# A two-block sequence model on one core: the order of weight splits and HGRN steps in the mixers

## The chip, the cores and the metric

One NeuronCore of a Trainium2 chip runs one launch of the kernel; the other cores are idle. The metric is the device time of that launch in microseconds. In the profile, PE is TensorE's matmul row, PEld its weight loads, DVE is VectorE, ACT is ScalarE, SP is SyncE, whose queue issues the DMAs. All arithmetic is fp32 in effect.

## The reference

The input is 256 tokens of width 1024. The reference applies a first block and then a second one. The first block has two layers, each a mixer and a gated feed-forward network; the second has a sparse-attention layer and a sliding-window layer, each with a feed-forward network as well. The change touches the mixer of the first block, which runs twice. It is, cut to what matters:

```python
p = rmsnorm(x) @ w_in                 # qkv, z, beta, a, hq, hf (2 directions), hi, gates
q, k, v = silu(dwconv(qkv)); q, k = l2norm(q) * 128**-0.5, l2norm(k)      # 4 heads of 128
# gated delta rule, forward and backward, chunks of tokens:
t_inv = inverse(eye + strict_lower(beta * k @ k.T * decay))
o_dn  = scan(t_inv @ (v * beta), t_inv @ (k * beta * exp(gc)), q @ k.T * decay, ...)
# HGRN2, forward and backward: S_t = diag(f_t) S_{t-1} + (1 - f_t) i_t^T, o_t = S_t^T q_t
o_hg  = scan(silu(hq), kk, hi, cumsum(logf))
merged = sigmoid(gate_dn) * (norm(o_dn) * silu(z) @ w_branch_dn) + sigmoid(gate_hg) * (norm(o_hg) * silu(hgate) @ w_branch_hg)
x = x + merged @ w_out
```

## The kernel before, in words

The kernel is written by hand, one instruction stream for each engine; each engine works strictly in the order written, and the streams meet at semaphores. TensorE counts finished groups in `P`, ScalarE its instructions in `A`, VectorE in `V`. PSUM is a ring of 8 banks (`Banks`): a group of matmuls takes the bank that was given back longest ago and waits until the results of its former owner have been read out of it.

**Weights.** All weights are streamed in tiles of 128 x 2048 fp32 (1 MB), in the order of `plan`. A tile passes through three steps. SP loads it into one of the raw buffers `RAW`. ScalarE casts it into a high half `WH` (`cp(half(WH, i), raw(i))`, L1100, recorded at the helper's line L1082). VectorE subtracts the high half from the raw tile, which gives the low half `WL` (L1687, recorded at L1659). TensorE then forms three products for each tile (high x high, high x low, low x high), in `feat`: 48 matmuls, about 6 us. `WH` and `WL` have three slots (`NWS`); the cast of tile i waits until TensorE is through with tile i - 3. On ScalarE and VectorE one call of `chunk()` does the next cast or subtraction in line, wherever in the stream it is written; ScalarE is one tile ahead of VectorE.

`RAW` has three slots, but from tile 16 to tile 29 of a mixer only two, since the third holds the gate projections `zg`. So tile 16 goes where tile 13 was, tile 17 where 15 was, tile 18 where 16 was, tile 19 where 17 was, and so on. SP issues the loads in order, each of them after the cast and the subtraction of the tile that it overwrites:

```python
elif j is not None:              # j = slot_former[i]
    w.wait_ge(*A["w hi", j])
    w.wait_ge(*V["w lo", j])
e.dma_start(raw(i), plan[i][0]).then_inc(*s_raw[slot[i]].up("raw", i))
```

The tiles of a mixer: 0 to 5 are qkv, 6 is narrow, 7 and 8 are `hq`, 9 to 12 are `f 0` to `f 3`, 13 and 14 are `it`, 15 to 18 are the projections `zp 0` to `zp 3`, from 19 on come the gates. The second mixer's tiles are the same plus 68.

**The head of the mixer.** TensorE projects `hq`, `f 0` and `f 1`; then come the small product `gc`, two groups of transposes `vt 0` and `vt 1`, and then four heads h, each with `kq h` (products of k and q with k), two groups `row h d`, which need `gB` and then a projection (`f 2`, `f 3`, `it 0`, `it 1`). The group `vt 1` is the next owner of the bank of `gc`. On ScalarE the inverse norms (`l2`, `rq`) are followed by a cast, by the logarithms of the forget gate (`logs(0)`) and the copies of `vt`. VectorE copies `gc`, forms `gB`, scales q and k (`unit(0)`, `unit(1)`), subtracts a tile, and then, head by head, masks (`dm`), forms the pairs, and runs `rest(h)`, a cumulative sum over the forget gate, whose last operations wait for ScalarE's `rest(h)`.

**The levels.** After fence f2 come six levels of a recursive triangular inverse on four groups g4 of 128 x 512 elements: TensorE multiplies (`y`), ScalarE copies, TensorE multiplies (`z`), and VectorE (to level 4) or ScalarE places the result with predicated copies and 32 x 32 transposes. Woven into these levels are 16 steps of HGRN, n = 0 to 15. Step n on VectorE is `hg_step(n)`: a predicated copy of the matmul result n (odd n only), the exponents of step n + 2 (`hg_exp`, two operations) and the product for step n + 1 (`hg_mul`, one or two operations), between which ScalarE takes the exponential. TensorE has a pair of matmul groups `hg` for odd n. `HG_STEPS` says how many steps lie in each level: two between and after the groups, any others at the end of the level. Levels 1 to 4 begin with a projection: TensorE runs `zp 0` before level 1 and `zp 1`, `zp 2`, `zp 3` at the ends of levels 1, 2 and 3; VectorE scales it in `zproj`. Tiles 17 to 21 are cast and tiles 16 to 20 subtracted in the calls of `chunk()` in this part.

Of the kernel before, what the change touches and what calls it, by code (L numbers as in the profile page):

```python
# [120 lines left out]
def program(nc, a):  # L121
    P_AT, P_W = par_layout()
    ctx = ExitStack()
    with ctx:
# [162 lines left out]
        XIv, XTv = (x.rearrange("p (g h n) -> p g h n", g=4, h=4) for x in (XI, XT))  # L287
        YBv = [y.rearrange("p (h n) -> p h n", h=4) for y in YBs]
        attv = att.rearrange("p (h s t) -> p h s t", h=4, s=2)
        HG_STEPS = (2, 2, 3, 3, 3, 3)  # L290
        HGI = [(kind, lv) for lv in (7, 0, 1, 2, 3, 4, 5, 6) for kind in range(2)]
        TM = [YBv[0], YBv[1]]
        vtv = vt.rearrange("p (j h n) -> p j h n", j=2, h=4)
# [780 lines left out]
        def scalar(e):  # L1074
# [12 lines left out]
            def waits(*pairs):  # L1087
                for s in pairs:
                    w.wait_ge(*s)
# [44 lines left out]
            def mixer(l):  # L1134
# [52 lines left out]
                def logs(c):  # L1187
                    E_, L1, L2 = HT[c % 2]
                    w.wait_ge(*V["f in", st, c])
                    act(E_, E_, ACT.Exp, "f exp", st, c)  # L1190
                    waits(A["f exp", st, c], *(f0 if c < 2 else [V["k out", st, c - 2]]))
                    act(L1, E_, ACT.Ln, "f l1", st, c, bias=1.0)
                    w.wait_ge(*V["lb"])
                    for j in range(2):
                        i = 2 * c + j
                        s1 = slice(j * 256, j * 256 + 256)
                        act(L2[:, s1], E_[:, s1], ACT.Ln, "f l2", st, c, bias=1.0, scale=LB[:, l * 8 + i:l * 8 + i + 1])

                def rest(c):
                    E_, L1, L2 = HT[c % 2]  # L1200
                    w.wait_ge(*V["f log", st, c])
                    act(L1, L1, ACT.Exp, "f inv", st, c, scale=-1.0)

                logs(0)
                for j in range(2):
                    w.wait_ge(*P["ps", st, "vt", j])
                    cp(vt[:, j * 512:j * 512 + 512], ps[st, "vt", j][:, :], "vt", st, j, of=ps.out(st, "vt", j))
                for h in range(4):
                    for d in range(2):
                        c = 4 * d + h  # L1210
                        dm = Dm[c % 2 + 2 * d]
                        major, minor = (slice(128, 384), slice(0, 128)) if d == 0 else (slice(0, 256), slice(256, 384))
                        waits(V["dm", st, h, d], V["bg", st])
                        act(dm[:, major], ps[st, "row", h, d][:, 0:256], ACT.Exp, "dm", st, h, d, bias=bg[:, d, c:c + 1],
                            of=ps.out(st, "row", h, d))
                        act(dm[:, minor], dm[:, minor], ACT.Exp, "dm", st, h, d, bias=lb_[:, 1 - d, c:c + 1])
                    if h == 0:
                        rest(0)
                    if h == 3:
                        for g4 in range(4):  # L1220
                            cp(XTv[:, g4], ident.unsqueeze(1).to_broadcast([128, 4, 128]), "ident", st, g4)
                    chunk()
                    if h >= 2:
                        c = h - 2
                        waits(P["ps", st, "it", c], V["rsT", st])
                        for j in range(2):
                            e.mul(v3(it, 2)[:, j, c * 256:c * 256 + 256], v3(ps[st, "it", c][:, :], 2)[:, j], rsT[:, j:j + 1]) \
                                .then_inc(*A.up("it", st, c, of=ps.out(st, "it", c)))
                    if h < 3:
                        logs(h + 1)  # L1230
                        rest(h + 1)
                A.note("f2", st)
                f2 = fence("f2", st)
                waits(*f2)

                def placed(out, src, kind, lv, *key, of):
                    for o, x in places(out, src, kind, lv):
# [49 lines left out]
                for lv in range(1, 7):  # L1287
                    for g4 in range(4):
                        dn_y(g4, lv)
                    if lv == 1:  # L1290
                        hg_diag()
                    hg_mm(n)
                    hg_exp(n + 2)
                    dn_z(0, lv)
                    dn_z(1, lv)
                    hg_mm(n + 1)
                    hg_exp(n + 3)
                    dn_z(2, lv)
                    dn_z(3, lv)
                    for m in range(2, HG_STEPS[lv - 1]):  # L1300
                        hg_mm(n + m)
                        hg_exp(n + m + 2)
                    n += HG_STEPS[lv - 1]
                    if lv < 5:
                        chunk()
                A.note("f3", st)
                f3 = fence("f3", st)
# [346 lines left out]
        def vector(e):  # L1654
# [117 lines left out]
            def mixer(l):  # L1772
# [37 lines left out]
                def forget(c):  # L1810
                    E_ = HT[c % 2][0]
                    waits(P["ps", st, "f", c, 0], *(f0 if c < 2 else [V["k out", st, c - 2]]))
                    stt(v3(E_, 2), v3(ps[st, "f", c, 0][:, :], 2), -1.0, rs2, ALU.mult, ALU.mult, "f neg", st, c, of=ps.out(st, "f", c, 0))
                    w.wait_ge(*V["f neg", st, c])
                    ts(E_, E_, 40.0, None, ALU.min, None, "f in", st, c)
# [16 lines left out]
                def unit(n):  # L1832
                    sx, sk = slice(n * 512, n * 512 + 512), slice(1024 + n * 512, 1536 + n * 512)
                    w.wait_ge(*A["rq", st, n])
                    stt(q_[:, sx], q_[:, sx], 128.0 ** -0.5, rq[:, sx], ALU.mult, ALU.mult, "q", st, n)
                    w.wait_ge(*A["rq", st, n + 2])
                    tt(k_[:, sx], k_[:, sx], rq[:, sk], ALU.mult, "k", st, n)
# [16 lines left out]
                tt(g_, gw2[:, :, 8:16], nea.unsqueeze(1).to_broadcast([128, 2, 8]), ALU.mult, "g", st)  # L1854
                ts(lb_, gw2[:, :, 0:8], -1.0, None, ALU.mult, None, "ln beta", st)
                forget(0)
                w.wait_ge(*P["ps", st, "gc"])
                cp(gc, v3(ps[st, "gc"][:, 0:16], 2), "gc", st, of=ps.out(st, "gc"))
                waits(V["gc", st], V["ln beta", st])
# [1 line left out]
                waits(V["g", st], *f0, *(P["ps", st, "l2", n] for n in range(4)))  # L1861
                for j in range(2):
                    cp(gB[:, j], g_[:, j, :].unsqueeze(2).to_broadcast([128, 8, 128]), "gB", st)
                unit(0)
                unit(1)
                chunk()
                e.memset(bb[:, :, 0:1], 0.0).then_inc(*V.up("bb0", st))

                for h in range(4):
                    if h < 3:  # L1870
                        forget(h + 1)
                    for d in range(2):
                        c = 4 * d + h
                        p, dm = ps[st, "row", h, d], Dm[c % 2 + 2 * d]
                        minor, ms, at, m1 = (slice(0, 128), slice(128, 256), 1, "MF") if d == 0 else \
                            (slice(256, 384), slice(0, 128), 0, "MB")
                        waits(P["ps", st, "row", h, d], V["gc", st], V["k", st, 1], *([V["pair", st, h - 2, d]] if h > 1 else []))
                        stt(dm[:, minor], p[:, ms], gc[:, at, c:c + 1], cn(m1), ALU.subtract, ALU.min, "dm", st, h, d,
                            of=ps.out(st, "row", h, d))
                    for d in range(2):  # L1880
                        c = 4 * d + h
                        dm, pg, pq = Dm[c % 2 + 2 * d], ps[st, "kk", h], ps[st, "kq", h]
                        o = slice(128, 512) if d == 0 else slice(0, 384)
                        b = slice(3, 6) if d == 0 else slice(0, 3)
                        waits(A["dm", st, h, d], P["ps", st, "kq", h])
                        stt(AT6[:, b, h], v3(pg[:, o], 3), -1.0, v3(dm, 3), ALU.mult, ALU.mult, "pair", st, h, d, of=ps.out(st, "kk", h))
                        tt(QKv[:, d, h], pq[:, o], dm, ALU.mult, "pair", st, h, d, of=ps.out(st, "kq", h))
                    if h == 0:
                        rest(0)
                    if h < 3:  # L1890
                        chunk()
                        rest(h + 1)
# [88 lines left out]
                tt(ZR[2], kk_[:, 0:1024], kk_[:, 1024:2048], ALU.add, "k sum", st)  # L1981
                hg_exp(0)
                hg_exp(1)
                hg_mul(0)
                chunk()

                def zproj(c):
                    scaled(zg[:, c * 512:c * 512 + 512], (st, "zp", c, 0), "zp", st, c)
# [6 lines left out]
                for lv in range(1, 7):  # L1995
                    if lv < 5:
                        zproj(lv - 1)
                    hg_step(n)
                    dn_z(0, lv)
                    dn_z(1, lv)  # L2000
                    hg_step(n + 1)
                    dn_z(2, lv)
                    dn_z(3, lv)
                    for m in range(2, HG_STEPS[lv - 1]):
                        hg_step(n + m)
                    n += HG_STEPS[lv - 1]
                    if lv < 5:
                        chunk()
                V.note("f3", st)
                f3 = fence("f3", st)  # L2010
# [646 lines left out]
```

## Time and profile before

| | |
|---|---|
| median of 3 runs | 1728.71 us (1727.83 to 1730.08) |
| the profiled execution | 1728.71 us, span 1726.9 us |
| TensorE busy | 95% of the span |
| VectorE busy | 72% |
| ScalarE busy | 56% |
| DMA | 246.11 MB, mean 143 GB/s |
| first mixer, head to level 6 | about 84 to 227 us |
| second mixer, the same | about 595 to 734 us |

The time of the execution lies 1.8 us above the span, which goes from the first to the last instruction. A row of the timeline has the start and the length in us, the engine, the line, the operation, the output and input by name (SA and SB are large scratch areas in SBUF, PS is PSUM, SM small vectors), the shapes, and the number of instructions of the same kind merged into it; in square brackets stands how long the engine was idle before it, and whose work ended the wait. Matmul rows overlap a little, since matmuls are pipelined.

### The profile page before, as it was taken

The numbers are of one execution on the slowest core, as the hardware profiler recorded it, in microseconds if no ns is written. First come the engines' busy times: TensorE is split into PE (matmuls) and PEld (weight loads), VectorE is DVE, ScalarE is ACT, GpSimd is POOL, SyncE is SP. The second block draws the span as 40 slices with busy tenths as digits, with TensorE's granted clock in tenths as the row PEclk, the third lists the DMA queues.
The fourth block names the chain that finished last, engine by engine and source line by source line (L and its number), as shares of the span: only waits on it lengthen the run. The fifth ranks groups of instructions, "written<-read, shape, count | busy, mean of one in ns | idle before, by whom it ended". The sixth has DMA issues, their size and how long they took to land.

```text
span 1726.9 us, 30663 instructions
## 1 busy us (share of the span) xinstructions
PE 1647.3 (95%) x13206; PEld 1597.1 (92%) x13206; DVE 1237.0 (72%) x1715; ACT 968.7 (56%) x1426; POOL 0.2 (0%) x4
## 2 busy tenths in 40 slices
PE   6999899999999999899999998999999998899997
PEld 6999899999999899899999996878999998799997
DVE  6889946777747789846777646766688748678863
ACT  6664455556536664565556542347577635567752
POOL 0000000000000000000000000000000000000000
PEclk9999999999999999999999999999999999999999
DMA  6421124455554312126555542520454543055551
GB/s 259 170 74 63 61 74 174 168 196 195 173 194 146 141 57 74 49 74 221 181 184 182 184 171 97 209 84 1 149 189 176 195 171 141 13 197 189 177 195 50
DMA packets 34983, 246.11 MB, mean 143 GB/s; under 512 B 3872, under 2 KB 4256, under 8 KB 5536
## 3 DMA queue, kind: packets, MB, share of 16 engines
q1 hardware_dynamic: 34848, 244.15, 39.8%
q8 instruction: 104, 1.70, 0.4%
q14 instruction: 31, 0.25, 0.0%
HBM read 243.09 MB, written 1.05 MB: 141 GB/s over the span
## 4 chain that ended last, share of the span: by engine, by line
PE 81%; DVE 13%; ACT 5%; issue 1%; DMA 0%; SPq 0%; DVEq 0%; ACTq 0%
PE PS L396 80%; DVE SA L1659 3%; DVE SB L1659 2%; ACT SB L1079 2%; DVE WL L1659 2%; DVE SB L1668 2%; ACT WH L1082 1%; DVE SB L1898 1%; PE PS L399 1%; DVE X L1659 1%; ACT XH L1122 0%; DVE SB L1663 0%; DMA RAW<-w_in 0%; DVE XL L1668 0%; DVE SA L1823 0%
## 5 line engine op out<-in xcount | busy, mean ns | idle before, releaser
L396 PE MATMUL PS<-XH,WH 128*128 128x256 f32 (+1 forms) x2536 | 725.3, 286 | 18.0 <-DVE WL L1659 17.3
L396 PE MATMUL PS<-XL,WH 128*128 128x256 f32 (+1 forms) x2536 | 717.6, 283 | 0.0
L396 PE MATMUL PS<-XH,WL 128*128 128x256 f32 (+1 forms) x2536 | 717.5, 283 | 0.0
L1082 ACT CAST WH<-RAW 128x2048 fp32r<-128x2048 f32 (+1 forms) x226 | 426.2, 1886 | 440.6 <-PE PS L396 391.5
L1659 DVE TENSOR_TENSOR WL<-RAW,WH 128x2048 fp32r<-128x2048 f32 (+1 forms) x226 | 510.9, 2261 | 159.5 <-ACT WH L1082 149.9
L396 PEld LDWEIGHTS PS<-XH,WH 128*128 128x128 f32 (+1 forms) x2536 | 484.6, 191 | 22.2 <-issue 18.1
L396 PEld LDWEIGHTS PS<-XL,WH 128*128 128x128 f32 (+1 forms) x2536 | 484.7, 191 | 2.6 <-issue 1.9
L396 PEld LDWEIGHTS PS<-XH,WL 128*128 128x128 f32 (+1 forms) x2536 | 484.6, 191 | 0.3
L396 PE MATMUL PS<-INH,WH 128*128 128x256 f32 x960 | 268.9, 280 | 1.1 <-DVE INL L1659 1.1
L396 PE MATMUL PS<-INH,WL 128*128 128x256 f32 x960 | 269.5, 281 | 0.0
L396 PE MATMUL PS<-INL,WH 128*128 128x256 f32 x960 | 267.0, 278 | 0.0
L396 PEld LDWEIGHTS PS<-INH,WH 128*128 128x128 f32 x960 | 180.5, 188 | 1.5 <-ACT INH L1082 1.5
L396 PEld LDWEIGHTS PS<-INL,WH 128*128 128x128 f32 x960 | 180.5, 188 | 0.0
L396 PEld LDWEIGHTS PS<-INH,WL 128*128 128x128 f32 x960 | 180.2, 188 | 0.0
L1659 DVE TENSOR_TENSOR SB<-PS,SM 128x512 f32<-128x512 f32 (+2 forms) x109 | 74.3, 682 | 85.5 <-PE PS L396 85.5
L1659 DVE TENSOR_TENSOR SB<-SB 128x512 f32<-128x512 f32 (+2 forms) x163 | 110.3, 677 | 12.3 <-ACT SB L1079 8.9
L396 PE MATMUL PS<-SA 128*128 128x128 f32 (+1 forms) x480 | 97.1, 346 | 18.8 <-DVE SA L1659 18.8
L396 PE MATMUL PS<-SB 128*128 128x128 f32 (+1 forms) x752 | 97.2, 285 | 9.9 <-ACT SB L1082 7.2
L1668 DVE SCALAR_TENSOR_TENSOR SB<-SB,PR 128x254 f32<-128x254 f32 (+2 forms) x212 | 95.6, 491 | 11.6 <-ACT SB L1079 8.0
L396 PEld LDWEIGHTS PS<-SB 128*128 128x128 f32 x752 | 91.0, 194 | 12.3 <-ACT SB L1082 11.3
L396 PEld LDWEIGHTS PS<-SA 128*128 128x128 f32 x480 | 70.0, 208 | 25.0 <-DVE SA L1659 16.2
L1082 ACT COPY SB<-PS 128x512 f32<-128x512 f32 (+4 forms) x156 | 68.3, 467 | 40.9 <-PE PS L396 39.1
(142 smaller groups left out, 1554.1 us busy)
## 6 DMA issues: line engine op xcount, KB each, us to landing
RAW<-w_in SPq DMA_DIRECT2D x52, 1024.0 KB, 4.9
RAW<-w_up SPq DMA_DIRECT2D x44, 1024.0 KB, 4.9
RAW<-f_in SPq DMA_DIRECT2D x44, 1024.0 KB, 4.8
RAW<-w_down SPq DMA_DIRECT2D x22, 1024.0 KB, 4.9
RAW<-f_out SPq DMA_DIRECT2D x22, 1024.0 KB, 4.8
RAW<-a_w_in SPq DMA_DIRECT2D x10, 1024.0 KB, 4.9
RAW<-w_out SPq DMA_DIRECT2D x8, 1024.0 KB, 4.9
RAW<-w_bdn SPq DMA_DIRECT2D x4, 1024.0 KB, 4.9
```

The lines of the kernel that those rows point to most:

```text
L396: return e.matmul(out, l, r, start=start, stop=stop, skip_group_check=True)
L399: return e.transpose(out, x, ident[0:k, 0:k])
L1079: e.activation(out, x, f, bias=bias, scale=scale).then_inc(*A.up(*key, of=of))
L1082: e.copy(out, x).then_inc(*A.up(*key, of=of))
L1659: e.tensor_tensor(out, x, y, op).then_inc(*V.up(*key, of=of))
L1668: e.scalar_tensor_tensor(out=out, in0=x, scalar=s, in1=y, op0=op0, op1=op1).then_inc(*V.up(*key, of=of))
L1898: e.copy_predicated(out, m, data).then_inc(*V.up(*key, of=of))
```

## The change

It moves calls within the streams of ScalarE and VectorE; no operation is added or removed on any engine. On ScalarE, `rest(0)` goes ahead of the `vt` copies, one `chunk()` goes from the end of level 4 to the place behind fence f2, and with it each cast from tile 18 to 21 is done one call earlier. On VectorE, `unit(0)`, `unit(1)` and their `chunk()` go ahead of the copy of `gc`, and `rest(0)` ahead of the loop over heads; `chunk()` comes before `hg_mul(0)` instead of after it, and the `chunk()` of the end of level 4 goes behind `zproj(0)` in level 1. `HG_STEPS` puts two steps into levels 3 and 4 and four into levels 5 and 6, on all three engines.

```diff
-        HG_STEPS = (2, 2, 3, 3, 3, 3)
+        HG_STEPS = (2, 2, 2, 2, 4, 4)
...
                 logs(0)                                     # ScalarE
+                rest(0)
                 for j in range(2):
                     w.wait_ge(*P["ps", st, "vt", j])
...
-                    if h == 0:
-                        rest(0)
...
                 f2 = fence("f2", st)
                 waits(*f2)
+                chunk()
...
                     n += HG_STEPS[lv - 1]
-                    if lv < 5:
+                    if lv < 4:
                         chunk()
...
                 forget(0)                                   # VectorE
+                unit(0)
+                unit(1)
+                chunk()
                 w.wait_ge(*P["ps", st, "gc"])
...
-                unit(0)
-                unit(1)
-                chunk()
                 e.memset(bb[:, :, 0:1], 0.0).then_inc(*V.up("bb0", st))
+
+                rest(0)
...
-                    if h == 0:
-                        rest(0)
...
                 hg_exp(0)
                 hg_exp(1)
+                chunk()
                 hg_mul(0)
-                chunk()
...
                         zproj(lv - 1)
+                    if lv == 1:
+                        chunk()
                     hg_step(n)
...
                     n += HG_STEPS[lv - 1]
-                    if lv < 5:
+                    if lv < 4:
                         chunk()
```

## Rows read from the trace of the kernel before

**Rows 1.** The page: busy us, share of the span and instructions of each engine.
```profile
PE 1647.3 (95%) x13206; PEld 1597.1 (92%) x13206; DVE 1237.0 (72%) x1715; ACT 968.7 (56%) x1426; POOL 0.2 (0%) x4
```

**Rows 2.** Windows: length, PE, PEld, DVE, ACT, POOL busy, clock, DMA share, GB/s.
```profile
150.00:175.00 25.00, 25.00 (x221) 25.00 (x220) 22.90 (x31) 9.78 (x13) 0.00 (x0) 1.00 0.24 85
191.90:226.70 34.80, 27.38 (x227) 27.05 (x227) 26.67 (x37) 18.03 (x37) 0.00 (x0) 0.95 0.10 31
699.90:734.40 34.50, 27.45 (x227) 27.07 (x227) 26.72 (x37) 18.04 (x37) 0.00 (x0) 0.95 0.09 31
```

**Rows 3.** SP's timeline and the DMA view (KB each, us to landing), 139 to 146 us: tile 18.
```profile
139.85 0.33 SPq L2498 DMA_DIRECT2D RAW<-w_in  x1
...
RAW<-w_in SPq DMA_DIRECT2D x1, 1024.0 KB, 4.7
```

**Rows 4.** VectorE's timeline: `hg_mul(0)`, tile 16, `zproj(0)`, one step; `hg_mul(0)`, second mixer.
```profile
136.27 0.69 DVE L1659 TENSOR_TENSOR SA<-SA 128x512 f32<-128x512 f32 x1
...
137.48 2.29 DVE L1659 TENSOR_TENSOR WL<-RAW,WH 128x2048 fp32r<-128x2048 f32 x1
139.69 0.69 DVE L1659 TENSOR_TENSOR RAW<-PS,SM 128x512 f32<-128x512 f32 x1
140.29 2.42 DVE L1659 TENSOR_TENSOR SA<-SA 128x512 f32<-128x512 f32 x3
...
645.59 0.69 DVE L1659 TENSOR_TENSOR SA<-SA 128x512 f32<-128x512 f32 x1
```

**Rows 5.** ScalarE's timeline, level 1: exponentials 0 and 1, and the cast of tile 18.
```profile
135.18 2.18 ACT L1079 ACTIVATE SA<-SA 128x1024 f32<-128x1024 f32 x2 [4.88 <-DVE SA L1659]
...
148.42 1.89 ACT L1082 CAST WH<-RAW 128x2048 fp32r<-128x2048 f32 x1
```

**Rows 6.** TensorE's timeline: level 1's first `z`, HGRN group 1, `zp 1`; the latter two, second mixer.
```profile
137.89 1.42 PE L396 MATMUL PS<-SB 128*128 128x128 f32 x8 [1.85 <-ACT SB L1082]
...
142.76 3.33 PE L396 MATMUL PS<-SA 128*128 128x128 f32 x16 [0.20 <-DVE SA L1659]
...
147.63 0.36 PE L396 MATMUL PS<-XH,WH 128*128 128x256 f32 x1
...
652.08 2.05 PE L396 MATMUL PS<-SA 128*128 128x128 f32 x16 [1.11 <-DVE SA L1659]
...
655.67 0.36 PE L396 MATMUL PS<-XH,WH 128*128 128x256 f32 x1
```

**Rows 7.** TensorE's timeline, head 0 of both mixers: `kq 0` and the start of `f 2`.
```profile
86.79 3.13 PE L396 MATMUL PS<-SA 128*128 128x256 f32 x8 [2.05 <-DVE SA L1659]
...
91.74 0.36 PE L396 MATMUL PS<-XH,WH 128*128 128x256 f32 x1
...
597.77 1.97 PE L396 MATMUL PS<-SA 128*128 128x256 f32 x8 [2.05 <-DVE SA L1659]
...
601.05 0.36 PE L396 MATMUL PS<-XH,WH 128*128 128x256 f32 x1
```

**Rows 8.** VectorE (`gc` copy, tile 12, head 1's `rest`) and ScalarE (last `rq`, both mixers).
```profile
83.85 0.17 DVE L1671 COPY SM<-PS 128x16 f32<-128x16 f32 x1 [2.22 <-PE PS L396]
...
87.77 2.28 DVE L1659 TENSOR_TENSOR WL<-RAW,WH 128x2048 fp32r<-128x2048 f32 x1
...
611.06 0.69 DVE L1659 TENSOR_TENSOR SB<-SB 128x512 f32<-128x512 f32 x1 [1.03 <-ACT SB L1079]
...
84.41 0.63 ACT L1079 ACTIVATE SB<-SB 128x512 f32<-128x512 f32 x1
...
594.61 0.63 ACT L1079 ACTIVATE SB<-SB 128x512 f32<-128x512 f32 x1
```

**Rows 9.** TensorE's timeline, first mixer: start of `zp 3`, HGRN groups 9 and 15.
```profile
176.99 0.36 PE L396 MATMUL PS<-XH,WH 128*128 128x256 f32 x1
...
196.68 3.65 PE L396 MATMUL PS<-SA 128*128 128x128 f32 x16 [4.77 <-DVE SA L1659]
...
224.68 2.02 PE L396 MATMUL PS<-SA 128*128 128x128 f32 x16 [0.87 <-DVE SA L1659]
```

## The prediction

> **What bounds the kernel now.** I read the page first: TensorE is busy for 1647.3 of 1726.9 us [rows 1], so only its 79.6 us of idle time can be won, and any new idle time is paid in full unless work is queued behind it. Then the table of windows; for the late levels of each mixer it has 34.80 us with 27.38 us busy and 34.50 us with 27.45 us busy, so 7.42 and 7.05 us idle, and a mean clock of 0.95, so part of each stretch ran at 1.2 instead of 2.4 GHz [rows 2]. The timelines say where: the heavy waits are one of 4.77 us for VectorE's product for HGRN group 9 and one of 0.87 us [rows 9]. Level 1 has waits too [rows 6], and so has the head of the mixer, 2.05 us each time [rows 7]. All the idle time that the edits can reach is in these three places. Between them TensorE has no wait (25.00 of 25.00 us busy in levels 2 and 3 [rows 2]), so a delay in one place reaches the end.
>
> **Part A, the head of the mixer (both `rest(0)`, the two `unit` calls and their `chunk()`).** Today TensorE waits 2.05 us for `k` of head 0 [rows 7]. With `unit(0)` first, `k` is ready in time: VectorE is idle there for 2.22 us, waiting for `gc` [rows 8]. But the low subtraction of tile 12 (2.28 us) now stands before the copy of `gc`. ScalarE ends the last `rq` at 84.41 + 0.63 = 85.04; then `k` (0.69, as the equally large operation in rows 4) gives 85.7, the subtraction 88.0, the copy of `gc` (0.17) 88.1 [rows 8]. The second `vt` transpose reuses the PSUM bank of `gc`, so TensorE waits for that copy and head 0's matmuls begin at about 88.5, not at 86.79. From there to the projection `f 2` it takes 601.05 - 597.77 = 3.28 us at the full clock (second mixer) and 91.74 - 86.79 = 4.95 us where the clock had fallen (first mixer) [rows 7]. At the full clock `f 2` would begin at 91.8 in the first mixer (before 91.74: +0.1) and, by the same sums from 594.61, at 602.0 in the second (before 601.05: +1.0). The new wait is some 3.8 us; waits of 2.05 us lowered the clock once in two cases [rows 7], waits of 4.77 us both times [rows 2, 9]. 3.8 is nearer to the second, so I add 4.95 - 3.28 = 1.67 us in both mixers: **+1.8 and +2.6, together +4.4 us**; bounds +1.1 and +4.4. VectorE cannot absorb it: its chain for head 1 waits for a cast that waits for `f 2`, with 1.03 us of idle time even now [rows 8]. The earlier `rest(0)` on both engines costs nothing more: its five VectorE operations only change places with the head-0 pairs, which TensorE needs two projections later, and the delayed `vt` copies are needed after `f 2`. If that cover were gone, it would be some 3 us.
>
> **Part B, level 1 (the new ScalarE `chunk()` behind fence f2, and on VectorE `chunk()` before `hg_mul(0)` and after `zproj(0)`).** The ScalarE call is the cast of tile 18. It waits for the load of tile 18. That load may start only when tile 16, which lies in the same raw buffer, has been cast and subtracted; today it is issued at 139.85, 0.08 us after the subtraction of tile 16 ends (137.48 + 2.29), and takes 4.7 us [rows 3, 4]. ScalarE now stands at this wait, and behind it in its queue are both first exponentials, the four `y` copies and the diagonal copies of level 1; TensorE's first level-1 `z` waits for the first `y` copy, VectorE's `hg_mul(0)` for the first exponential.
> Step by step, first mixer. VectorE is free for tile 16 where `hg_mul(0)` began, 136.27 [rows 4]; subtraction (2.29) to 138.5; load issued 138.6, landed 143.3; cast 1.89 to 145.2; the two exponentials 2.18 to 147.3 [rows 5]. Today `z` starts 137.89 - 137.36 = 0.53 us after the exponentials [rows 5, 6]: now at 147.8, **9.9 us later**. VectorE: first exponential 146.2, `hg_mul(0)` 1.3 to 147.5, `zproj(0)` to 148.1, the subtraction of tile 17, now in front, to 150.3, the next step (2.42) to 152.7 [rows 4]. HGRN group 1 starts at 152.7 instead of 142.76, **+9.9 us**, and it is this that decides when projection 1 starts. Second mixer: `hg_mul(0)` began at 645.59, so 152.7 - 136.27 = 16.4 gives 662.0 against 652.08, +9.9 [rows 4, 6].
> From group 1 to projection 1 it takes 655.67 - 652.08 = 3.59 us at full clock and 147.63 - 142.76 = 4.87 us at the low one [rows 6]. After an idle stretch of 12 us and another of 2 to 3 us the clock is low; a burst after a long wait lost 1.67 us in part A's rows, and I take this again. First mixer: 9.9 + 3.59 + 1.67 - 4.87 = +10.3. Second: 9.9 + 1.67 = +11.6. **Part B: +21.9 us**; bounds +18.6 (full clock) and +25.2 (the loss twice in each).
> Levels 2 and 3 give nothing back: TensorE is never idle there [rows 2]. ScalarE's casts 19, 20 and 21, now one level early, wait until the projection before has released their high buffer, but the `y` copies behind them are still in time for `z`, by about 1 us. If that were wrong, each level would lose up to 2 us.
>
> **Part C, levels 4 to 6 (`HG_STEPS`, `chunk()` only to level 3).** Let Z be the start of projection 3, 176.99 today; the last HGRN pair ends at 224.68 + 1.8 = Z + 49.5 [rows 9]. New order: level 4 has no group 9 and VectorE no third step and no subtraction. TensorE ends level 4 at Z + 14.8 (no wait). VectorE ends its level-4 placings of groups 2 and 3 at Z + 17.7 and 19.1, and `y` of level 5 waits for them: 1.6 us idle. Four `z` pairs and HGRN group 9 run to Z + 29.0 with no wait (its product is ready at Z + 22.3). Group 11 needs three VectorE steps after group 9 has been copied: at 2.42 us a step [rows 4] ready at Z + 31.1, 2.1 us idle. Level 6: `y` waits 0.2 us behind ScalarE's exponential 13, group 13 0.3 us, and group 15 waits for the predicated copies of group 13 and for one and a half steps (3.6), ready at Z + 45.1, 2.8 us idle. End Z + 47.0: a gain of 2.5 us; 2.2 us in the second mixer, which has 0.37 us less to lose [rows 2]. No single wait exceeds 3 us, so I let the clock stand. **Part C: -4.7 us**; bounds -6.7 (1 us more in each) and -1.3 (1.67 us for the clock in each).
>
> **Sum.** 4.4 + 21.9 - 4.7 = +21.6 us. The profiled execution took 1728.71 us (span 1726.9), which is also the median of the three runs: **1750.3 us**. All low ends: 1.1 + 18.6 - 6.7 = +13.0, 1741.7; all high ends: 4.4 + 25.2 - 1.3 = +28.3, 1757.0.
>
> **What the Trainium skill adds.** Its page "DMA: Bandwidth & Descriptors" (section on the anatomy of one DMA) says that DMA engines do not wait on semaphores: the issuing sequencer waits before dispatch. The trace agrees: the load goes out 0.08 us behind the subtraction [rows 3, 4], and it speaks against part B, since nothing can prefetch tile 18. Its formula, 2.0 us plus bytes over 436e3, gives an estimate of 4.4 us for 1 MB where the trace has 4.7; with it the sum would be 0.6 us less.
> The page "TensorE: Matmul & The Clock Gate" (section on HAM oscillation) says that a burst after a wait for data starts at half clock each time. The trace agrees for both waits of 4.77 us and for only one of the two of 2.05 us; its result stands as the third rival.
>
> **The rivals.**
> 1. *Not slower: tile 18 is there in time.* If the load had landed before ScalarE comes to it (about 130 us), the cast would lie in 4.88 us of idle time [rows 5] and part B would be only the subtraction moved in front of group 1: 2.1 us in each mixer, less 1.3 us if the first keeps its clock. 4.4 + 2.9 to 4.2 - 4.7 = +3 to +4; with part A at its low end 0 to 1: **1729 to 1732**. The point that decides is whether the load can be issued 8 us earlier; rows 3 and 4 tie it to tile 16. 3%.
> 2. *The new step split removes all waits of levels 4 to 6.* Then part C is -(7.4 + 7.1) and some 3.3 for the clock, -17.8: **1737**. Against it: VectorE needs its steps one after another between two HGRN groups. 4%.
> 3. *The clock falls at every new wait.* Part B at its high end and 1.67 us twice more in each part C: 4.4 + 25.2 - 1.3 + 3.3 = +31.6: **1760**. For it: 0.95 in rows 2. 8%.
> 4. *The late casts delay the `y` copies in levels 2 to 4*, 1 to 2 us in each of six: **1758**. 3%.
> My own forecast (1742 to 1757) has the other 82%.
>
> **Numbers.** Differences under 0.2% (3.5 us) are about what a measurement of this kernel cannot tell from none. Faster: 1% (case 1 with a better part C). Within: 3%. Slower: 96%. Range 1741 to 1757: it leaves out the cases 1 to 4 for the most part, and takes in the bounds of the sum.
>
> **What would show it.** In the trace after: a ScalarE wait for a DMA of the raw tile of about 8 us or more before the cast that follows fence f2, in both mixers; the first level-1 `z` some 11.5 us after the diagonal matmuls, with half clock there; the load for tile 18 right behind a subtraction that ends 1.3 us earlier than today relative to the placings; a TensorE wait of about 3.8 us between the `vt` transposes, and none for `k`; the wait of 4.77 us gone, with waits of 1 to 3 us at `y` of level 5 and before groups 11 and 15. The prediction is wrong if the cast starts without a wait, if the wait is hidden because TensorE has other matmuls queued, or if levels 2 and 3 make up for it.

## The result and the profile after

The changed kernel takes **1757.45 us** in the median of 4 runs (1754.54 to 1761.98), the kernel before 1728.57 us (1727.83 to 1730.08): a ratio of 1.0168 [1.0144, 1.0193], so 28.9 us slower where 21.6 were forecast. That is 0.45 us above the range. The profiled execution took 1757.52 us, 28.8 more than that of before; all differences below are made between these two. The page of the kernel after has this line of busy times:

```profile
PE 1651.7 (94%) x13206; PEld 1600.4 (91%) x13206; DVE 1237.5 (70%) x1715; ACT 969.2 (55%) x1426; POOL 0.2 (0%) x4
```

Beside [rows 1] TensorE has 4.4 us more busy time and the same instructions, and the span is 28.8 us longer: the other 24.4 us are idle time of TensorE. The view of waits by what ended them names the new ones (us in total, times, longest):

```profile
PE PS L396 <- ACT WH L1082: 29.9, 2, 15.0
...
PE PS L399 <- DVE SM L1671: 6.8, 2, 3.8
...
PE PS L396 <- DVE SB L1898: 2.3, 4, 0.9
```

None of the three is among the waits of before. The first is TensorE's wait for a *cast*, in level 1 of each mixer. To see where the time went, I take the starts of a few operations in both traces; a stage's cost is how much later its last landmark comes in the kernel after than in the kernel before, less the same for its first. A is from `f 1` to `f 2`, B from `f 2` to `zp 1`, C from `zp 3` to HGRN group 15, the last one of level 6. For the first mixer B is (162.08 - 93.92) - (147.63 - 91.74) = 12.27 with the rows below and [rows 6, 7]; C is (236.63 - 224.68) - (191.43 - 176.99) = -2.49 [rows 9]. In us:

| part | mixer 1 | mixer 2 | sum | forecast |
|---|---|---|---|---|
| A | +1.54 | +2.64 | +4.2 | +4.4 |
| B | +12.27 | +13.75 | +26.0 | +21.9 |
| levels 2 and 3 | 0.0 | 0.0 | 0.0 | 0 |
| C | -2.49 | -2.10 | -4.6 | -4.7 |
| all the rest | | | +3.2 | 0 |

Part B is where the forecast lost its size. The table of windows (columns as in [rows 2]) covers level 1, from the end of `zp 0` to `zp 1`: first both mixers of the kernel before, then both of the kernel after.

```profile
130.50:147.60 17.10, 13.85 (x96) 13.10 (x96) 16.28 (x23) 7.40 (x12) 0.00 (x0) 0.80 0.16 62
640.00:655.60 15.60, 11.16 (x95) 10.62 (x95) 15.50 (x21) 7.26 (x11) 0.00 (x0) 1.00 0.19 68
```

```profile
132.70:162.10 29.40, 13.69 (x98) 13.46 (x97) 18.00 (x23) 9.55 (x12) 0.00 (x0) 0.71 0.19 72
...
654.50:684.00 29.50, 13.86 (x97) 13.69 (x97) 17.90 (x23) 9.55 (x12) 0.00 (x0) 0.71 0.20 72
```

The busy time is that of before in the first mixer and 2.7 us more in the second (there the clock was full, 1.00); TensorE's idle time rose from 3.3 to 15.7 us and from 4.4 to 15.6 us. The timelines of level 1 in the kernel after, SyncE's load of tile 18 with its DMA row, then ScalarE and VectorE:

```profile
140.72 0.33 SPq L2500 DMA_DIRECT2D RAW<-w_in  x1
...
RAW<-w_in SPq DMA_DIRECT2D x1, 1024.0 KB, 4.8
```

```profile
145.70 1.90 ACT L1082 CAST WH<-RAW 128x2048 fp32r<-128x2048 f32 x1 [13.22 <-DMA RAW<-w_in]
147.50 2.00 ACT L1079 ACTIVATE SA<-SA 128x1024 f32<-128x1024 f32 x2
```

```profile
138.36 2.29 DVE L1659 TENSOR_TENSOR WL<-RAW,WH 128x2048 fp32r<-128x2048 f32 x1
148.59 1.29 DVE L1659 TENSOR_TENSOR SA<-SA 128x512 f32<-128x512 f32 x2 [7.94 <-ACT SA L1079]
...
150.40 2.28 DVE L1659 TENSOR_TENSOR WL<-RAW,WH 128x2048 fp32r<-128x2048 f32 x1
156.00 2.43 DVE L1659 TENSOR_TENSOR SA<-SA 128x512 f32<-128x512 f32 x3 [3.32 <-PE PS L396]
```

TensorE in the same stretch, then the same places of the second mixer:

```profile
147.74 6.43 PE L396 MATMUL PS<-SB 128*128 128x128 f32 x32 [14.98 <-ACT WH L1082]
154.01 1.95 PE L396 MATMUL PS<-SA 128*128 128x128 f32 x16
155.80 1.95 PE L396 MATMUL PS<-SB 128*128 128x128 f32 x16
158.48 2.05 PE L396 MATMUL PS<-SA 128*128 128x128 f32 x16 [0.73 <-DVE SA L1659]
...
162.08 0.36 PE L396 MATMUL PS<-XH,WH 128*128 128x256 f32 x1
...
669.41 6.70 PE L396 MATMUL PS<-SB 128*128 128x128 f32 x32 [14.91 <-ACT WH L1082]
...
684.02 0.36 PE L396 MATMUL PS<-XH,WH 128*128 128x256 f32 x1
```

Read them from the load on. VectorE ends the subtraction of tile 16 at 138.36 + 2.29 = 140.65, SyncE issues the load of tile 18 at 140.72, it lands some 4.8 us later, and the cast starts at 145.70 after 13.22 us of idle time: this chain is the forecast, step by step (138.5, 138.6, 143.3, each plus the 2.2 us by which the first mixer already ran late). TensorE is the surprise. It should have formed the four `y` groups (the 32 matmuls) and the two diagonal groups (16) right after `zp 0`, at 132.8, and waited at the first `z`. It waited *before the first `y`*, until 147.74, just behind the cast's end at 147.60. So 5.6 us of matmuls (by f1_note's rows below, 132.63 to 138.23), which in the kernel before lie beside VectorE's and ScalarE's work, now stand behind the cast, and the 32 run at a low clock: they take 6.43 us instead of 3.81. VectorE, which had done its subtraction by 152.68, waits for the diagonal groups (154.01 + 1.95 = 155.96) until 156.00, since its next step overwrites what they read, and group 1 follows that step.

The wait is in the program text. TensorE's `y` of level 1 waits for the "placed" marks of level 0, of VectorE and of ScalarE. On ScalarE, which places nothing at level 0, the mark is only a note: it records how many counted instructions stand above it in ScalarE's stream, and whoever waits for the mark waits until ScalarE has done that many. The note is written below the new `chunk()`:

```python
w.wait_ge(*A["placed", st, g4, lv, side])   # TensorE, before y of level lv + 1
...
waits(*f2)                                  # ScalarE
chunk()                                     # new: cast of tile 18
...
for g4 in range(4):
    for side in range(2):
        A.note("placed", st, g4, 0, side)   # counts the cast too
hg_exp(0)
```

### The profile page after: what moved, and what is told of

It reads as the page before. It is cut to its first block, busy times and chain, and to the rows that moved or that the text cites. A ratio compares the mean times of both kernels' runs of the same rounds, so it can differ in the third digit from the quotient of the medians.

```text
span 1755.7 us, 30675 instructions
## 1 busy us (share of the span) xinstructions
PE 1651.7 (94%) x13206; PEld 1600.4 (91%) x13206; DVE 1237.5 (70%) x1715; ACT 969.2 (55%) x1426; POOL 0.2 (0%) x4
## 4 chain that ended last, share of the span: by engine, by line
PE 79%; DVE 13%; ACT 6%; issue 1%; DMA 1%; SPq 0%; DVEq 0%; ACTq 0%
PE PS L396 78%; DVE SA L1659 3%; ACT SB L1079 2%; DVE WL L1659 2%; DVE SB L1659 2%; DVE SB L1668 1%; ACT WH L1082 1%; DVE SB L1898 1%; PE PS L399 1%; ACT XH L1122 1%; DMA RAW<-w_in 1%; DVE X L1659 1%; DVE SB L1902 0%; DVE SB L1663 0%; DVE SA L1823 0%
## 5 line engine op out<-in xcount | busy, mean ns | idle before, releaser
L396 PE MATMUL PS<-SB 128*128 128x128 f32 (+1 forms) x752 | 100.8, 293 | 32.4 <-ACT WH L1082 29.9
L396 PEld LDWEIGHTS PS<-SB 128*128 128x128 f32 x752 | 94.9, 202 | 34.8 <-issue 30.2
L1659 DVE TENSOR_TENSOR SB<-SB 128x512 f32<-128x512 f32 (+2 forms) x163 | 110.4, 677 | 18.6 <-ACT SB L1079 15.2
L1659 DVE TENSOR_TENSOR SA<-SA 128x512 f32<-128x512 f32 (+1 forms) x114 | 80.2, 766 | 22.7 <-ACT SA L1079 15.8
```

The source lines that it names most:

```text
L396: return e.matmul(out, l, r, start=start, stop=stop, skip_group_check=True)
L1659: e.tensor_tensor(out, x, y, op).then_inc(*V.up(*key, of=of))
```

## The experiments

Each kernel ran beside the kernel before on the same chip. The first four share one set of runs of it (median 1728.96 us, 19 runs, 1726.93 to 1733.89), the last four another (1730.35 us, 20 runs, 1728.06 to 1733.46).

**1. f1_note: is it the note?** The changed kernel with the notes moved ahead of the cast, nothing else.

```diff
                 waits(*f2)
+                for g4 in range(4):
+                    for side in range(2):
+                        A.note("placed", st, g4, 0, side)
                 chunk()
...
-                for g4 in range(4):
-                    for side in range(2):
-                        A.note("placed", st, g4, 0, side)
                 hg_exp(0)
```

> The changed kernel with the bookkeeping loop that notes level 0 as placed on ScalarE put ahead of the new cast instead of behind it; no instruction is moved. Theory N (the y groups wait for the cast of tile 18 only because the note counts it): y and the diagonal products run right after zp 0, before the long wait; the long TensorE idle stretch stands before the first z; HGRN group 1 starts where VectorE lets it, 2.4 us after the subtraction of tile 17, some 3.4 us earlier than in the changed kernel in each mixer, zp 1 1.7 to 3.4 us earlier because the low clock now falls on other groups: 1751 to 1754. Rival R (the length of the stall is set by the transfer and the low clock alone, whatever lies in front of it): no change, 1757 plus or minus 2.

Measured: 1748.11 us (1746.85 to 1755.09, 4 runs), ratio 1.0114 [1.0084, 1.0144], 9.3 us below the kernel after. TensorE's timeline, level 1, and the end of it in the second mixer; then VectorE's step ahead of group 1:

```profile
132.63 3.81 PE L396 MATMUL PS<-SB 128*128 128x128 f32 x32
136.28 1.95 PE L396 MATMUL PS<-SA 128*128 128x128 f32 x16
149.89 3.60 PE L396 MATMUL PS<-SB 128*128 128x128 f32 x16 [11.66 <-ACT SB L1082]
154.94 2.05 PE L396 MATMUL PS<-SA 128*128 128x128 f32 x16 [1.45 <-DVE SA L1659]
...
158.53 0.36 PE L396 MATMUL PS<-XH,WH 128*128 128x256 f32 x1
...
673.16 2.05 PE L396 MATMUL PS<-SA 128*128 128x128 f32 x16 [1.27 <-DVE SA L1659]
...
676.76 0.36 PE L396 MATMUL PS<-XH,WH 128*128 128x256 f32 x1
```

```profile
152.46 2.42 DVE L1659 TENSOR_TENSOR SA<-SA 128x512 f32<-128x512 f32 x3
```

This is the picture that the prediction drew: `y` and diagonals at once, 11.66 us of waiting at the first `z`, group 1 at 154.94. It had 152.7, and the mixer was 2.2 us late: 154.9. B is 8.73 and 10.03 us here, 3.54 and 3.72 less than with the note in its place; rival R is out. The gain is larger than was expected: the two profiled executions are 10.2 us apart, of which 7.3 are B's and 2.8 lie where nothing was edited (the rest, up to the last matmuls, is -0.6 us here and +2.2 us there). From group 1 to `zp 1` it takes 158.53 - 154.94 = 3.59 us, the time at the full clock: the clock was low only for the two `z` groups (3.60 us for 16 matmuls instead of 1.95), and that delays nothing, since VectorE's step for group 1 ends later (154.88) than they do (153.49). So the 1.67 us that I had added in each mixer is not there. In the kernel after a low clock is on the path, but in another place: the 32 `y` matmuls, 6.43 us instead of 3.81, stand ahead of the diagonal groups. So some 2.6 of the 3.54 us are the clock of the displaced `y` groups and the other 0.9 their place; this split is an estimate from these rows.

**2. f2_head: part A alone.** Only the moves of `rest(0)`, `unit(0)`, `unit(1)` and their `chunk()`.

> The kernel before with part A alone (both rest(0), unit(0), unit(1) and their chunk() ahead of the gc copy). By the sum of the prediction +1.1 to +4.4; by the trace of the changed kernel (+1.6 and +2.6) +4.2: 1732.8. Rival: the head's shift is absorbed later, since VectorE has slack before head 1: 1729.

Measured: 1734.92 us (1732.01 to 1737.53, 10 runs), ratio 1.0032 [1.0021, 1.0042]; A is +1.38 and +2.64 us, with 3.80 us before `vt 1`. In the trace part A costs by itself what it costs in the whole, 4.0 us, and nothing of it is absorbed later. The median is 6.0 us above that of the kernel before; the profiled execution (1732.01 us) is the fastest of the ten, and where the others lose 2 us more is not known.

**3. f3_cast: part B alone**, with the steps as before.

```diff
                 waits(*f2)
+                chunk()                     # ScalarE; and its call at level 4 goes
...
                 hg_exp(1)
+                chunk()                     # VectorE
                 hg_mul(0)
-                chunk()
...
+                    if lv == 1:
+                        chunk()             # its call at level 4 goes
```

> The kernel before with part B alone (the cast behind fence f2, the chunk() calls of VectorE in level 1, none at the end of level 4), with the old HG_STEPS. If part B carries the loss: +12.3 and +13.8 as in the changed kernel, less about 2 us in each mixer because the subtraction and the cast at the end of level 4 are gone: +22, 1751. Rival (the parts hurt each other and B alone is small): below 1740.

Measured: 1753.92 us (1752.54 to 1755.52, 4 runs), ratio 1.0135 [1.0117, 1.0154]; B is +12.51 and +12.78, C -2.04 and -1.69 us. TensorE's timeline has the same wait:

```profile
146.04 6.72 PE L396 MATMUL PS<-SB 128*128 128x128 f32 x32 [14.92 <-ACT WH L1082]
```

Part B costs its 25.3 us in level 1 without any help from parts A and C, and the rival is out. A of the second mixer came out +2.96 us although nothing is edited there: `kq 0` ran at the low clock behind its wait of 2.05 us, as in g8_late below. That C gains here too, 3.7 us, was expected (about 2 us in each mixer, for the cast and the subtraction that leave the end of level 4); the rows point to the cast. In levels 4 to 6 its timeline has the waits before groups 9 and 15 as before:

```profile
209.73 3.35 PE L396 MATMUL PS<-SA 128*128 128x128 f32 x16 [4.77 <-DVE SA L1660]
...
235.68 2.02 PE L396 MATMUL PS<-SA 128*128 128x128 f32 x16 [0.86 <-DVE SA L1660]
```

What is gone is a third wait, 1.78 us in the kernel before, at the first `z` of level 5 behind ScalarE's `y` copy. TensorE's row, and ScalarE's row of the cast right ahead of that copy, both of the kernel before:

```profile
205.68 3.84 PE L396 MATMUL PS<-SB 128*128 128x128 f32 x32 [1.78 <-ACT SB L1082]
```

```profile
203.26 1.88 ACT L1082 CAST WH<-RAW 128x2048 fp32r<-128x2048 f32 x1
```

In f3_cast that cast is done a call earlier, at the end of level 3, and the copies start 0.1 us before the exponential's end by the records (216.01 against 215.05 + 1.06). So a gain of part C's kind comes without `HG_STEPS` too.

**4. f4_steps: `HG_STEPS` alone.**

> The kernel before with HG_STEPS (2, 2, 2, 2, 4, 4) alone. The wait of 4.77 us for group 9 goes, but the subtraction (2.25 us) still stands at the end of level 4 and delays all of level 5: 2.5 minus 2.25 is 0.2 us won in each mixer: 1728.2, no change that can be told. Rival (the step split alone brings the gain of part C): 1724.

Measured: 1732.58 us (1729.12 to 1735.66, 10 runs), ratio 1.0014 [1.0001, 1.0027]. Its timeline, HGRN groups 9, 11 and 15, and windows (columns as in [rows 2]) behind the start of group 15 and in the second mixer's level 1:

```profile
203.05 2.05 PE L396 MATMUL PS<-SA 128*128 128x128 f32 x16 [0.53 <-DVE SA L1659]
...
210.68 2.02 PE L396 MATMUL PS<-SA 128*128 128x128 f32 x16 [2.01 <-DVE SA L1659]
...
224.81 2.54 PE L396 MATMUL PS<-SA 128*128 128x128 f32 x16 [2.65 <-DVE SA L1659]
```

```profile
224.00:230.00 6.00, 5.20 (x32) 5.23 (x33) 0.66 (x1) 2.12 (x6) 0.00 (x0) 0.72 0.00 0
647.00:651.00 4.00, 1.84 (x10) 1.40 (x8) 4.00 (x5) 3.94 (x8) 0.00 (x0) 0.80 0.00 0
```

The wait of 4.77 us [rows 9] is gone, and waits of 0.53, 2.01 and 2.65 us stand in its place; C is -1.67 and -0.19 us up to the start of group 15, but -0.04 and +1.28 up to the product two groups behind it. For here the clock fell behind group 15's wait in both mixers, and also in a stretch of level 1 where nothing had been edited and where it was 1.00 before. The new split by itself gives no gain that can be measured: no change was expected, and the rival (1724) is out.

**5. g5_same17: is it the load?** The changed kernel without the load of tile 18: the cast and the subtraction read the buffer of tile 17 again.

```diff
+            if i - 18 in MIXERS:
+                s = slot[i - 1]             # tile 18 takes the buffer of tile 17
             slot.append(s)
...
             def load(i):
+                if i - 18 in MIXERS:
+                    s_raw[slot[i]].note("raw", i)
+                    return
```

> The changed kernel, but tile 18 of each mixer is not loaded: its cast and subtraction read the raw tile 17 again, so zp 3 multiplies with the weights of zp 2, and 1 MB less is moved in each mixer. The cast behind fence f2 stays where it is. Theory (the stall is the cast's wait for a transfer that cannot start before tile 16 is subtracted): the cast runs in ScalarE's idle time right after zp 0, y starts 1 to 2 us late, group 1 of HGRN waits only for the subtraction that was put in front (2.1 us), levels 4 to 6 keep their gain: +4.2 + 2.9 to 4.2 - 4.6, 1731 to 1733. Rival (a cast in front of the exponentials is what costs, transfer or not): above 1740.

Measured: 1735.91 us (1735.3 to 1740.76, 4 runs), ratio 1.0042 [1.0027, 1.0057]. TensorE's timeline:

```profile
134.76 5.44 PE L398 MATMUL PS<-SB 128*128 128x128 f32 x32 [2.15 <-ACT WH L1084]
...
146.89 3.41 PE L398 MATMUL PS<-SA 128*128 128x128 f32 x16 [3.12 <-DVE SA L1661]
...
151.85 0.36 PE L398 MATMUL PS<-XH,WH 128*128 128x256 f32 x1
```

Both places of `chunk()` and the note are as in the kernel after. SyncE still issues a load behind the subtraction of tile 16, at 140.57, but it is that of tile 19, and the cast waits for none: what is gone is the cast's wait for a transfer, and with it 21.5 us. The rival (above 1740) is out. B falls to +2.21 and +3.63 us: TensorE waits 2.15 us for the cast itself (1.90 long) at the first `y`, through the note, and 3.12 us before group 1, behind the subtraction of tile 17. That is 5.8 us where 2.9 to 4.2 were expected, here and in the prediction's first rival; that rival failed on its condition, since the load could not be early.

**6. to 8. Does anything of the change pay?** g7_unit0 moves `unit(0)` alone ahead of the copy of `gc`. g8_late has the new `HG_STEPS` and puts VectorE's level-4 subtraction behind the first step of level 5; ScalarE's calls stay. g6_both has both edits.

```diff
+                unit(0)                     # g7, g6 (VectorE, ahead of the gc copy)
                 w.wait_ge(*P["ps", st, "gc"])
...
-                unit(0)
                 unit(1)
...
                     hg_step(n)
+                    if lv == 5:             # g8, g6 (VectorE)
+                        chunk()
...
-                    if lv < 5:
+                    if lv < 4:
                         chunk()
```

> A version built from what the runs showed: unit(0) alone ahead of the copy of gc, HG_STEPS (2, 2, 2, 2, 4, 4), and of the calls of chunk() only VectorE's at the end of level 4, which goes behind the first step of level 5, where VectorE waited 2.7 us for group 9. The gains of the next two kernels add: 1718 to 1720. Rival (other stages or the clock take it back): 1725 or above.

> The kernel before with unit(0) alone ahead of the copy of gc. The wait of 2.05 us for k goes and no new one comes, since gc and gB are copied before the subtraction: f 2 starts 2.2 us earlier in each mixer, 3.8 where the clock had fallen, and VectorE follows with 2.2 and 3.5: 1723. Rival (VectorE bounds the heads and takes it back): 1727.

> The kernel before with HG_STEPS (2, 2, 2, 2, 4, 4) and VectorE's chunk() of the end of level 4 behind the first step of level 5. The subtraction (2.25 us) lies in the wait for group 9 (2.7 us), so part C's gain comes without part B: -2.5 and -2.1, 1724. Rival (as for the steps alone: the gain inside the levels is lost again): 1728 to 1732.

Measured: g7_unit0 1725.59 us (1724.26 to 1726.78, 8 runs), ratio 0.9973 [0.9963, 0.9983]; g8_late 1729.38 us (1726.07 to 1733.44, 12 runs), ratio 0.9995 [0.9986, 1.0004]; g6_both **1722.08 us** (1721.03 to 1723.88, 5 runs), ratio 0.9955 [0.9943, 0.9966]. g7_unit0 and g6_both are faster than the kernel before, by 4.8 and 8.3 us; g8_late is not, and with it its rival (1728 to 1732) came true and not the 1724 that were expected. The 1718 to 1720 for g6_both were missed by 2 us. TensorE's `kq 0` in g6_both (first mixer) and in g8_late (second mixer):

```profile
84.61 1.89 PE L396 MATMUL PS<-SA 128*128 128x256 f32 x8
```

```profile
598.25 3.75 PE L396 MATMUL PS<-SA 128*128 128x256 f32 x8 [2.05 <-DVE SA L1659]
```

With `unit(0)` alone in front the copy of `gc` is still in time: no wait before `kq 0`, none before `vt 1`, A is -3.96 and -2.29 us. In g8_late C is -2.46 and -2.09 us, exactly as in the kernel after, although the cast of ScalarE still stands at the end of level 4. But the profiled execution is the slowest of the twelve (1733.44 us): the second `kq 0`, whose wait of 2.05 us is that of before [rows 7], ran at the low clock this time, and A of the second mixer, where nothing is edited, came out +2.90 us. The gain is in the stage and not in the median. In g6_both the wait before `kq 0` is gone, and the two edits together give 8.3 us, more than the 4.8 and 1.0 us (the latter within the noise) that they give apart. That this surplus comes from the missing wait is an argument; no run separates it.

## Why the prediction came out as it did

**Part A: right in mechanism, and in size by two terms that partly cancel.** TensorE's and VectorE's timelines of the kernel after:

```profile
88.73 1.12 PE L399 MATMUL PS<-C,SA 128*128 128x128 f32 x4 [3.79 <-DVE SM L1671]
89.64 2.96 PE L396 MATMUL PS<-SA 128*128 128x256 f32 x8
...
93.92 0.36 PE L396 MATMUL PS<-XH,WH 128*128 128x256 f32 x1
...
610.27 0.81 PE L399 MATMUL PS<-C,SA 128*128 128x128 f32 x4 [3.02 <-DVE SM L1671]
610.88 3.46 PE L396 MATMUL PS<-SA 128*128 128x256 f32 x8
...
615.65 0.36 PE L396 MATMUL PS<-XH,WH 128*128 128x256 f32 x1
```

```profile
86.31 2.29 DVE L1659 TENSOR_TENSOR WL<-RAW,WH 128x2048 fp32r<-128x2048 f32 x1
88.51 0.17 DVE L1671 COPY SM<-PS 128x16 f32<-128x16 f32 x1
```

The subtraction stands in front of the copy of `gc`, and `vt 1` waits 3.79 us for it. Behind this wait the clock was low in both mixers, as assumed (mean 0.83 and 0.82 over the head). Forecast were +1.8 and +2.6 us, measured are +1.54 and +2.64. In the first mixer, which already ran 0.64 us late, `kq 0` began 0.5 us later than forecast (89.64 - 0.64 = 89.0 against 88.5), and from there to `f 2` it took 4.28 us where I had taken 4.95. The cover of the later `vt` copies held.

**Part B: the chain of the cast was right, the list of what stands behind it was not.** The failed step is the sentence on what stands behind ScalarE's wait: "behind it in its queue" both exponentials, the `y` copies and the diagonal copies, so that TensorE is held at the first `z`. That is true of the queue of ScalarE, and I took TensorE to be held only by those. It is also held by counts: the note for "placed" of level 0 counts every instruction of ScalarE written above it. So TensorE stood before the first `y` (14.98 and 14.91 us) and not at the first `z`, and f1_note shows the price, 3.54 and 3.72 us. I had read the rows of level 1 in which `y` runs on ahead of the exponentials, but not asked what the count in its wait would hold once an instruction was put above the note. The second failed step has the other sign: 1.67 us for the clock in each mixer, which f1_note shows not to be on the path from group 1 on, since the low clock covered only `z` groups that VectorE's step outlasts. Without it the forecast is 21.9 - 3.3 = 18.6 us, and f1_note has 18.8: that is the test of the chain. With the 7.3 us that the note was measured to cost it makes 25.9; measured are 26.0. The two errors have opposite signs, and that part B missed by 4.1 us and not by 7.3 is luck.

**Levels 2 and 3: right.** They give back nothing and cost nothing (0.0 us in every kernel), and level 4 has no wait either, so the fourth rival (casts that delay the `y` copies, 1758 us) is out, though its time is within 1 us of the measured one (its own terms, 1 to 2 us in each of six levels, give 1756 to 1762).

**Part C: right in size, its parts only in part shown.** The timeline of the kernel after (`y` of level 5 twice, HGRN groups 11 and 15, and group 15 of the second mixer) and the window from `zp 3` to behind group 15:

```profile
209.06 1.16 PE L396 MATMUL PS<-SB 128*128 128x128 f32 x8 [0.92 <-DVE SB L1898]
210.42 4.73 PE L396 MATMUL PS<-SB 128*128 128x128 f32 x40 [0.20 <-DVE SB L1898]
...
222.52 2.02 PE L396 MATMUL PS<-SA 128*128 128x128 f32 x16 [2.01 <-DVE SA L1659]
...
236.63 2.02 PE L396 MATMUL PS<-SA 128*128 128x128 f32 x16 [2.65 <-DVE SA L1659]
...
758.59 2.02 PE L396 MATMUL PS<-SA 128*128 128x128 f32 x16 [2.65 <-DVE SA L1659]
```

```profile
191.40:238.50 47.10, 41.20 (x356) 40.27 (x355) 38.81 (x55) 23.38 (x44) 0.00 (x0) 1.00 0.06 23
```

Forecast were 1.6, 2.1 and 2.8 us before `y`, group 11 and group 15; they are 1.12 (0.92 + 0.20), 2.01 and 2.65. The sum of the two mixers is -4.6 us where -4.7 were forecast. The prediction's reading of before left out a wait: 4.77 and 0.87 are 5.64 of the 7.42 us of idle time, and the other 1.78 us are the wait at the first `z` of level 5 behind ScalarE's cast. It did not spoil the sum, which was worked forward from `zp 3`. But three edits meet here: `HG_STEPS` alone gives nothing that lasts (f4_steps), the earlier casts and subtractions alone 3.7 us (f3_cast), and the steps with the late subtraction the whole (g8_late), so the gains do not add up edit by edit. The second rival (all these waits vanish, 1737 us) is out. So is the third (a low clock after every new wait, 1760 us): the window's clock is 1.00 behind waits of up to 2.65 us.

The Trainium skill's page "TensorE: Matmul & The Clock Gate" (section on HAM oscillation) has each burst of its example start at half clock behind a wait for a transfer. Its waits are longer than those of part C, which the prediction did not say. Part A (waits of 3.79 and 3.02 us) and level 1 (14.98 and 14.91 us) agree; part C, with 1.00 behind waits of up to 2.65 us, is not that case. Nor is a short wait safe: see the table at the end.

**The rest, 3.2 us.** The sum had nothing for stages in which no instruction is moved. This is the third failed step, a term put at nothing. The profiled execution has +0.64 us there before the first edited place, +1.6 us in the sparse-attention layer and +0.9 us from the last matmuls on. The same operations come at a higher or lower clock from one kernel to the next: the sparse-attention layer is +1.6 in the kernel after, -1.5 in f1_note and +1.65 in g8_late. What decides this was not found. Without it the prediction would have been off by little more than the 4.1 us of part B.

## What to carry to other kernels

A count on a semaphore that is taken down by a note, without an instruction of its own, holds everything written above it in that queue: before moving an instruction up, look for the notes it passes and for who waits on them, not only for the instructions behind it. A cast that is moved ahead of the moment at which its buffer can be refilled starts only when the refill has landed, and everything behind it waits with it: here 13.22 us, of which the transfer is 4.8. The test is the issue time of the load, which here is tied to the end of another engine's work. Charge a low clock only to matmuls that the end waits for: in f1_note 16 matmuls took 3.60 us instead of 1.95 and delayed nothing. And read the edits of a bundle apart: one of its moves (`unit(0)` alone) and its `HG_STEPS`, with a later place for one subtraction, give 8.3 us together, hidden under 30 us of loss.

## What the runs showed of the hardware

The granted clock after a short wait is not a property of the place, and of the two waits under 3 us the longer one lowered it less often. Over all profiled executions, both mixers counted, this is how often the matmuls right behind a wait ran at the low clock:

| wait of TensorE | us | low clock behind it | kernels |
|---|---|---|---|
| before `kq 0` | 2.05 | 6 of 8 (2.42 to 3.75 us instead of 1.97) | before, f3_cast, f4_steps, g8_late |
| before HGRN group 15 | 2.65 | 3 of 12 (2.54 to 3.50 us instead of 2.02) | after, f1_note, f4_steps, g5_same17, g6_both, g8_late |
| before `vt 1` | 3.0 to 3.8 | 8 of 8 (`kq 0` took 2.8 to 3.5 us instead of 1.89) | after, f1_note, f2_head, g5_same17 |
| before HGRN group 9 | 4.77 | 8 of 8 (3.3 to 3.8 us instead of 1.95) | before, f2_head, f3_cast, g7_unit0 |

In f4_steps the clock fell to 0.80 between 647 and 651 us, in a stretch of unedited code. Such a fall moved the end of its stage by some 1.5 to 3.0 us, as much as an edit here is worth. This fits what the medians show: g8_late is better by 4.5 us inside the edited levels and cannot be told from the kernel before. Its five runs with a mean clock of 0.989 took 1726.07 to 1727.58 us, its seven with 0.984 to 0.986 took 1729.29 to 1733.44. The kernel before alone scatters over 7.0 us in 19 runs. After 15 us without work the clock fell in both mixers, and the mean over level 1 was 0.71 both times, against 0.80 and 1.00 in the kernel before (the windows of level 1 above).
